# First norm and first modulation group of a hybrid encoder layer: x loaded ahead of the weights, the group summed on TensorE

## The chip, the cores and the metric

One core of a Trainium2 chip runs the kernel; the other seven are idle. The metric is the device time in microseconds, median over runs. Everything is float32 in and out, batch 1, 512 tokens, width 2048.

## The reference, cut to what matters

Only the head of the layer is touched by the change: a modulation vector from c, a normed and modulated copy of x, and the input projection.

```python
mod = silu(c) @ w_ada[l] + b_ada[l]                     # 2048 -> 6 * 2048
sh1, sc1, g1, sh2, sc2, g2 = jnp.split(mod, 6, axis=-1)
h = rms_norm(x, norm_mix_pre[l]) * (1.0 + sc1) + sh1
proj = h @ w_in[l]                                      # then attention heads and HGRN2 heads
...
x = x + g1 * rms_norm(mix, norm_mix_post[l])
h = rms_norm(x, norm_ffn_pre[l]) * (1.0 + sc2) + sh2    # then the convolution FFN
```

For the first norm only sh1 and sc1 are needed: the first 4096 columns of w_ada, 33.5 MB. The gates and the second pair are made later, beside other work.

## The kernel before, in words

All five engines run programs written out by hand; semaphores order them. h is held transposed: 16 row tiles kt of 128 model channels by 512 tokens. A float32 product is made of three passes on TensorE (`three_passes`, L2032 to L2034): each operand is split into a high part (ScalarE copies to a rounded type, lines L742, L776) and a low part (VectorE subtracts, lines L1359, L1355).

**The head of the kernel ("front").** SyncE's queue issues, in order, the rows of w_ada's first 4096 columns (`load_ada`), 16 weight rows w_in of 448 KB (`load_front`), and, between rows 2 to 5 of the first group, the four 1 MB tiles of x. The columns are taken in groups of row tiles, `MOD_GROUPS = ((0, 6), (6, 4), (10, 4), (14, 2))`: group g makes the shift and the scale of its row tiles. A group comes as 16 loads, one for each 128 rows of w_ada. For each, VectorE does ACC = w_ada row * silu(c) + ACC (`add_ada`, L1337 and L1340). After the sixteenth, TensorE sums ACC over its 128 partitions with a matmul against a column of ones for each 128 columns (`sum_ada`, L2027), VectorE adds the bias and forms the scale (`modulate`, L1348, L1350), ScalarE applies both to the transposed x (XN) and makes H_hi (`h_rows`, L772, L776), VectorE makes H_lo (`h_low`, L1355).

**x.** ScalarE squares the four tiles of x (L750), takes the root through Ln and Exp (L752, L753), scales the tiles (L758). TensorE then turns all of x (`turn_x`, L2009, 64 transposes), and ScalarE copies each of the 16 turned row tiles out of PSUM (L763).

**The front rows.** TensorE runs `front_row(kt)` for 16 row tiles, 7 column tiles of three passes each, 21 matmuls of 128x512, with `sum_ada(g)` one row before the first row that needs group g:

```python
sum_ada(0)
for kt in range(KT):
    for g in range(1, len(MOD_GROUPS)):
        if kt == MOD_GROUPS[g][0] - 1:
            sum_ada(g)
    front_row(kt)
```

Five projections of query heads follow at once, then the HGRN2 heads, the output projection and the FFN, all led by TensorE. The raw front weights stand in two slots (W_raw), which come free when VectorE has made the low part. The constants that a reader needs: KT = 16 (row tiles and w_ada rows), TT = 4 (token tiles), RAW = 2 (raw slots), SLOTS = 4 (split weight slots), U_Q = 16 (first unit after the front).

Of the kernel before, what the change touches and what calls it, by code (L numbers as in the profile page):

```python
# [69 lines left out]
MOD_GROUPS = ((0, 6), (6, 4), (10, 4), (14, 2))  # L70
# [80 lines left out]
def hybrid_encoder_layer(nc, x, c, w_ada, b_ada, norm_mix_pre, norm_mix_post, w_in, q_norm, k_norm,  # L151
# [6 lines left out]
    def at(name, shape, dt, offset):  # L158
# [20 lines left out]
    ADA1 = at("ADA1", [P, ADA1_SLOTS, 12 * P], F32, 8 * KB)  # L179
    ADA2 = at("ADA2", [P, ADA2_SLOTS, 8 * P], F32, WK + 32 * KB)  # L180
    ACC = [at("ACC0", [P, 12 * P], F32, WK + 56 * KB), at("ACC1", [P, 8 * P], F32, 56 * KB),
           at("ACC2", [P, 8 * P], F32, WK + 56 * KB), at("ACC3", [P, 4 * P], F32, WK + 62 * KB)]
# [100 lines left out]
    with ExitStack() as ctx:  # L283
# [16 lines left out]
        ada2_landed = [sem(f"ada2_landed{i}") for i in range(ADA2_SLOTS)]  # L300
        ada_added, mod_summed, mod_ready = sem("ada_added"), sem("mod_summed"), sem("mod_ready")
# [78 lines left out]
        OUT_BANKS = [[0, 1, 6, 7], [2, 3, 4, 5]]  # L380

# [68 lines left out]
        def _(sp):  # L450
# [11 lines left out]
            def load_ada(g, r):  # L462

                n = g * KT + r
                row0, rows = MOD_GROUPS[g]
                if g == 0:
                    dst, landed = ADA1[:, r % ADA1_SLOTS, :], ada1_landed[r % ADA1_SLOTS]
                    if r >= ADA1_SLOTS:
                        sp.wait_ge(ada_added, n - ADA1_SLOTS + 1)
                else:  # L470
                    slot = (n - KT) % ADA2_SLOTS
                    dst, landed = ADA2[:, slot, 0:2 * rows * P], ada2_landed[slot]
                    if n - KT >= ADA2_SLOTS:
                        sp.wait_ge(ada_added, n - ADA2_SLOTS + 1)
                sp.dma_start(dst.rearrange("p (s n) -> p s n", s=2),
                             w_ada[0, r * P:(r + 1) * P, 0:2 * D].rearrange("p (s n) -> p s n", s=2)
                             [:, :, row0 * P:(row0 + rows) * P]).then_inc(landed, 16)

            def load_front(u):
                if u >= RAW:  # L480
                    sp.wait_ge(lo_ready, u - RAW + 1)
                sp.dma_start(W_raw[:, u % RAW, 0:FRONT_W], w_in[0, u * P:(u + 1) * P, FRONT_COL:FRONT_COL + FRONT_W])\
                    .then_inc(raw_landed[u % RAW], 16)
# [5 lines left out]
            front = {(0, 0): 0, (0, 1): 1, (0, 9): 2, (0, 10): 3, (1, 0): 4, (1, 1): 5, (1, 13): 6, (1, 15): 7,  # L489
                     (2, 2): 8, (2, 5): 9, (2, 12): 10, (2, 15): 11, (3, 4): 12, (3, 6): 13, (3, 12): 14, (3, 15): 15}  # L490
            for g in range(len(MOD_GROUPS)):
                for r in range(KT):
# [3 lines left out]
                    if g == 0 and 2 <= r < 2 + TT:  # L496
                        sp.dma_start(XT0[:, r - 2, :], x[0, (r - 2) * P:(r - 1) * P, :]).then_inc(x_landed[r - 2], 16)
# [223 lines left out]
        def _(act):  # L721
# [16 lines left out]
            def split_front(u):  # L738
# [3 lines left out]
                act.activation(W_hi[:, u % SLOTS, 0:FRONT_W], W_raw[:, u % RAW, 0:FRONT_W], ACT.Copy).then_inc(hi_ready, 1)  # L742
# [3 lines left out]
            split_front(0)  # L746
            split_front(1)
# [8 lines left out]
            act.wait_ge(x_rstd, 1)  # L756
            for tt in range(TT):
                act.activation(XT0[:, tt, :], XT0[:, tt, :], ACT.Copy, scale=col(SM, RSX + tt)).then_inc(x_scaled, 1)  # L758
                if tt in (1, 3):
                    split_front(2 + tt // 2)  # L760
            for dt in range(KT):
                act.wait_ge(x_turned, dt + 1)
                act.activation(XN[:, dt, :], PB[dt % 4][:, :], ACT.Copy).then_inc(xn_ready, 1)  # L763
# [15 lines left out]
            for u in range(4, 9):  # L779
                split_front(u)  # L780
            h_rows(1)
            for u in range(9, 12):
                split_front(u)
            h_rows(2)
            for u in range(12, 16):
                split_front(u)
            h_rows(3)
            split_hi(0, 2, U_Q)
# [494 lines left out]
        def _(dve):  # L1283
# [14 lines left out]
            dve.memset(col(SM, EPSC), EPS)  # L1298
            dve.memset(CT[:, :], 0.0).then_inc(c_zeroed, 1)
# [24 lines left out]
            def add_ada(g, r):  # L1324

                n = g * KT + r
                if g == 0:
                    src = ADA1[:, r % ADA1_SLOTS, :]
                    dve.wait_ge(ada1_landed[r % ADA1_SLOTS], 16 * (r // ADA1_SLOTS + 1))
                else:  # L1330
                    slot = (n - KT) % ADA2_SLOTS
                    src = ADA2[:, slot, 0:2 * P * MOD_GROUPS[g][1]]
                    dve.wait_ge(ada2_landed[slot], 16 * ((n - KT) // ADA2_SLOTS + 1))
                if r == 0:
                    if g == 2:
                        dve.wait_ge(mod_summed, 1)
# [20 lines left out]
            def front_low(u):  # L1357
                dve.wait_ge(hi_ready, u + 1)
                dve.tensor_tensor(W_lo[:, u % SLOTS, 0:FRONT_W], W_raw[:, u % RAW, 0:FRONT_W],  # L1359
                                  W_hi[:, u % SLOTS, 0:FRONT_W].bitcast(F32), ALU.subtract).then_inc(lo_ready, 1)  # L1360

            for r in range(KT):
                add_ada(0, r)
                if r == 2:
                    vectors()
                if r in (3, 4):
                    front_low(r - 3)
                if r == 10:
                    lower_bounds()
                if r in (12, 14):  # L1370
                    front_low(r // 2 - 4)
            for r in range(KT):
# [3 lines left out]
                if 1 <= r <= 6:  # L1376
                    h_low(r - 1)
                if r in (7, 9, 12, 15):
                    front_low(4 + (7, 9, 12, 15).index(r))
            for r in range(KT):  # L1380
# [614 lines left out]
        def _(pe):  # L1995
# [3 lines left out]
            pe.transpose(PB[2][:, 0:P], CT[:, :], ident[:, :]).then_inc(c_turned, 1)  # L1999
            pe.wait_ge(stage_landed, 17 * 16)  # L2000
# [3 lines left out]

            def turn_x(dt):
                if dt >= 4:
                    pe.wait_ge(xn_ready, dt - 3)
                for tt in range(TT):
                    ins = pe.transpose(PB[dt % 4][:, tt * P:(tt + 1) * P], XT0[:, tt, dt * P:(dt + 1) * P], ident[:, :])  # L2009
                ins.then_inc(x_turned, 1)  # L2010

            pe.wait_ge(c_ready, 1)
            pe.wait_ge(vec_ready, 1)
            pe.wait_ge(x_scaled, TT)
            for dt in range(KT):
# [113 lines left out]
            sum_ada(0)  # L2129
# [400 lines left out]
```

## Time and profile before

| | us |
|---|---|
| median of 3 runs (2381.16 to 2386.85) | 2384.36 |
| the profiled execution | 2380.28 |
| its span, first to last instruction | 2378.5 |
| TensorE busy in the span | 2303.4 (97%) |
| VectorE busy | 1863.6 (78%) |
| ScalarE busy | 1101.8 (46%) |

How to read it: PE is TensorE (PEld its weight loads), DVE VectorE, ACT ScalarE, SP the queue of SyncE. Times within the span are us from its first instruction. "Busy" counts an instruction from start to end, so overlapping ones share time.

### The profile page before, as it was taken

Reading aid. Unit: us, or ns where it says so; the run is one execution under the profiler, and the core shown is the slowest. Engines: PE = TensorE matmul, PEld = TensorE weight load, DVE = VectorE, ACT = ScalarE, POOL = GpSimd, SP = SyncE. Lnnn points to the kernel's source line nnn. Section 1 sums busy time; section 2 is a strip of 40 time slices with the busy share of each in tenths; the row PEclk is TensorE's granted clock in tenths of the full one; section 3 lists DMA queues with packets and bytes.
Section 4 is the critical chain, followed back from the end, with each engine's and each line's share of the span. In section 5 each row is a group of like instructions: output and inputs, shape, how many; then the busy total and the mean of one; then the engine's idle time right before and its main releaser. Section 6 shows DMA issues by size and latency. Waiting matters only on the chain.

```text
span 2378.5 us, 36941 instructions
## 1 busy us (share of the span) xinstructions
PE 2303.4 (97%) x13613; PEld 2026.8 (85%) x13613; DVE 1863.6 (78%) x2393; ACT 1101.8 (46%) x1495; POOL 129.3 (5%) x207
## 2 busy tenths in 40 slices
PE   2899999999999999989999999999999999999998
PEld 2777778888888887878999999999999998888887
DVE  6965667876767872267799999999999999889777
ACT  5356753333333352254444444444444445555554
POOL 1010000000000000000000000000000000001100
PEclk9999999999999999999999999999999999999999
DMA  9952456766666734336555555555555569769966
GB/s 370 335 157 72 145 176 199 226 221 210 207 218 186 238 92 174 98 124 155 143 146 146 144 142 143 143 139 141 144 145 142 142 175 327 254 206 291 273 227 223
DMA packets 374480, 442.46 MB, mean 186 GB/s; under 512 B 14620, under 2 KB 291364, under 8 KB 372096
## 3 DMA queue, kind: packets, MB, share of 16 engines
q1 hardware_dynamic: 354704, 369.74, 48.9%
q0 software_dynamic: 19696, 71.68, 13.1%
q8 instruction: 46, 0.75, 0.1%
q14 instruction: 34, 0.28, 0.0%
HBM read 418.81 MB, written 66.08 MB: 204 GB/s over the span
## 4 chain that ended last, share of the span: by engine, by line
PE 92%; DVE 4%; ACT 2%; DMA 1%; issue 1%; SPq 0%; DVEq 0%; ACTq 0%
PE bank L2032 28%; PE bank L2034 27%; PE bank L2033 27%; PE bank L2189 2%; DMA ADA<-in_w_ada_dram 1%; PE bank L2098 1%; PE bank L2221 1%; DVE ACC L1340 1%; PE bank L2208 1%; PE bank L2089 1%; PE bank L2251 1%; DVE W_lo L1294 0%; PE bank L2027 0%; DVE ZZ L1528 0%; PE bank L2347 0%
## 5 line engine op out<-in xcount | busy, mean ns | idle before, releaser
L2032 PE MATMUL bank<-H_lo,W_hi 128*128 128x256 f32 (+1 forms) x1888 | 659.7, 349 | 3.3 <-DVE H_lo L1355 3.3
L2034 PE MATMUL bank<-H_hi,W_lo 128*128 128x256 f32 (+1 forms) x1888 | 635.0, 336 | 0.0
L2033 PE MATMUL bank<-H_hi,W_hi 128*128 128x256 f32 (+1 forms) x1888 | 634.6, 336 | 0.0
L2032 PEld LDWEIGHTS bank<-H_lo,W_hi 128*128 128x128 f32 x1888 | 359.8, 191 | 42.7 <-issue 7.7
L2033 PEld LDWEIGHTS bank<-H_hi,W_hi 128*128 128x128 f32 x1888 | 359.9, 191 | 39.4 <-issue 7.7
L2034 PEld LDWEIGHTS bank<-H_hi,W_lo 128*128 128x128 f32 x1888 | 359.0, 190 | 37.6
L2032 PE MATMUL bank<-T_lo,W_hi 128*128 128x256 f32 x1280 | 362.3, 283 | 0.0
L2033 PE MATMUL bank<-MGR,W_hi 128*128 128x256 f32 x1280 | 362.2, 283 | 0.0
L2034 PE MATMUL bank<-MGR,W_lo 128*128 128x256 f32 x1280 | 362.2, 283 | 0.0
L1294 DVE TENSOR_TENSOR W_lo<-W_raw,W_hi 128x1024 fp32r<-128x1024 f32 x138 | 168.3, 1221 | 110.4 <-ACT W_hi L735 110.0
L2032 PEld LDWEIGHTS bank<-T_lo,W_hi 128*128 128x128 f32 x1280 | 245.7, 192 | 0.1
L2033 PEld LDWEIGHTS bank<-MGR,W_hi 128*128 128x128 f32 x1280 | 245.7, 192 | 0.0
L2034 PEld LDWEIGHTS bank<-MGR,W_lo 128*128 128x128 f32 x1280 | 245.7, 192 | 0.0
L2032 PE MATMUL bank<-W_lo,GS_hi 128*128 128x512 f32 x616 | 240.0, 390 | 1.6 <-DVE W_lo L1882 1.6
L2033 PE MATMUL bank<-W_hi,GS_hi 128*128 128x512 f32 x616 | 239.7, 389 | 0.0
L2034 PE MATMUL bank<-W_hi,GS_lo 128*128 128x512 f32 x616 | 239.6, 389 | 0.0
L1130 ACT ACTIVATE W_hi<-UB 128x1024 fp32r<-128x1024 f32 x160 | 164.1, 1049 | 148.6 <-DVE UB L1751 95.1
L1739 DVE TENSOR_TENSOR W_lo<-UB,W_hi 128x1024 fp32r<-128x1024 f32 x160 | 195.0, 1220 | 26.9 <-ACT W_hi L1130 26.9
L735 ACT ACTIVATE W_hi<-W_raw 128x1024 fp32r<-128x1024 f32 x138 | 144.8, 1050 | 93.9 <-PE bank L2034 44.3
L1577 DVE SCALAR_TENSOR_TENSOR AB_acc<-AB_raw,SM,AB_acc 128x1024 f32<-128x1024 f32 x120 | 153.7, 1281 | 23.1 <-DMA AB_raw<-in_w_ada_dram 22.1
L1130 ACT ACTIVATE W_hi<-W_raw 128x1024 fp32r<-128x1024 f32 x80 | 84.5, 1056 | 150.6 <-DVE W_raw L1751 98.3
L2032 PEld LDWEIGHTS bank<-W_lo,GS_hi 128*128 128x128 f32 x616 | 115.7, 188 | 26.8 <-DVE W_lo L1882 2.5
(280 smaller groups left out, 3603.4 us busy)
## 6 DMA issues: line engine op xcount, KB each, us to landing
AB_raw<-in_w_ada_dram SPq DMA_DIRECT2D x128, 512.0 KB, 4.5
UB<-in_w_up_dram SPq DMA_DIRECT2D x100, 512.0 KB, 4.1
W_raw<-in_w_in_dram SPq DMA_DIRECT2D x90, 512.0 KB, 4.7
t_dram<-in_w_down_dram POOLq DMA_DIRECT2D x88, 512.0 KB, 7.9
DRAW<-in_w_down_dram SPq DMA_DIRECT2D x66, 512.0 KB, 6.1
W_raw<-in_w_up_dram SPq DMA_DIRECT2D x56, 512.0 KB, 3.9
W_raw<-in_w_down_dram SPq DMA_DIRECT2D x44, 512.0 KB, 6.1
ADA<-in_w_ada_dram SPq DMA_DIRECT2D x32, 512.0 KB, 6.3
```

Of the source, the lines that this page charges most:

```text
L735: act.activation(W_hi[:, k % SLOTS, :], W_raw[:, k % RAW, :], ACT.Copy).then_inc(hi_ready, 1)
L1130: act.activation(units(W_hi[:, (U_ST + PRODUCTS * jj + p) % SLOTS, :]), ST[e][ST_UNIT[p]], ACT.Copy)\
L1294: dve.tensor_tensor(W_lo[:, k % SLOTS, :], W_raw[:, k % RAW, :], W_hi[:, k % SLOTS, :].bitcast(F32), ALU.subtract).then_inc(lo_ready, 1)
L1340: ins = dve.scalar_tensor_tensor(ACC[g][:, :], src, col(SM, CS + r), ACC[g][:, :], ALU.mult, ALU.add)
L1577: ins = dve.scalar_tensor_tensor(AB_acc[:, :], AB_raw[:, kt % 2, :], col(SM, CS + kt), AB_acc[:, :], ALU.mult, ALU.add)
L1739: dve.tensor_tensor(units(W_lo[:, slot, :]), ST[e][ST_UNIT[p]], units(W_hi[:, slot, :].bitcast(F32)), ALU.subtract)\
L2032: pe.matmul(acc, st_hi, mv_lo, start=start, stop=False, skip_group_check=on)
L2033: pe.matmul(acc, st_hi, mv_hi, start=False, stop=False, skip_group_check=on)
L2034: return pe.matmul(acc, st_lo, mv_hi, start=False, stop=stop, skip_group_check=on)
L2089: ins = pe.transpose(PB[6 + qt % 2][:, k * P:(k + 1) * P], PM[qt][:, k * P:(k + 1) * P], ident[:, :])
L2098: ins = pe.matmul(PB[2][:, :], VSA[:, k, :], PT[:, k, :], start=(k == 0), stop=(k == TT - 1))
L2189: ins = pe.matmul(bank[:, a * P:(a + 1) * P], KM[:, a * P:(a + 1) * P], queries, start=True, stop=True)
```

## The change

Five groups in place of four: row tiles (4, 4, 4, 2, 2). The first group is no longer added up by VectorE: for each of its 16 w_ada rows, TensorE multiplies the row's 8 column blocks, as stationary operands, by the matching column of silu(c), and accumulates into 8 columns of PSUM bank 7 (`ada_row`), which a matmul with zeros has opened. The rows 8 to 15 alternate with the transposes of x. VectorE adds only groups 1 to 4. x is loaded ahead of all w_ada rows. VectorE scales x, where ScalarE did. ScalarE's two splits of front units 2 and 3 come behind its copies of the turned x. The raw front weights 2 to 13 have places of their own (FRAW), and their loads wait for the high part of two units before; unit 6 waits for all transposes.

```diff
-MOD_GROUPS = ((0, 6), (6, 4), (10, 4), (14, 2))
+MOD_GROUPS = ((0, 4), (4, 4), (8, 4), (12, 2), (14, 2))
...
     def load_ada(g, r):
-        n = g * KT + r
+        n = (g - 1) * KT + r
         if g == 0:
             if r >= ADA1_SLOTS:
-                sp.wait_ge(ada_added, n - ADA1_SLOTS + 1)
+                sp.wait_ge(ada_used, r - ADA1_SLOTS + 1)
...
     def load_front(u):
         if u >= RAW:
-            sp.wait_ge(lo_ready, u - RAW + 1)
+            sp.wait_ge(hi_ready, u - RAW + 1)
+        if u == RAW + 4:
+            sp.wait_ge(x_turned, KT)
+        if u >= RAW + len(FRAW):
+            sp.wait_ge(lo_ready, u % RAW + 1)
...
+    for tt in range(TT):
+        sp.dma_start(XT0[:, tt, :], x[0, tt * P:(tt + 1) * P, :]).then_inc(x_landed[tt], 16)
+    front = {(0, 0): 0, (0, 1): 1, (0, 10): 2, (0, 12): 3, (1, 4): 4, (1, 5): 5, (1, 9): 6, (1, 13): 7,
+             (2, 0): 8, (2, 8): 9, (2, 11): 10, (2, 14): 11, (3, 2): 12, (3, 8): 13, (3, 14): 14, (4, 5): 15}
...
 ScalarE
-    split_front(0)
-    split_front(1)
+    act.activation(col(SM, RSX), col(SM, EPSC), ACT.Ln)
...
     act.activation(SM[:, RSX:RSX + TT], SM[:, RSX:RSX + TT], ACT.Exp, scale=-0.5).then_inc(x_rstd, 1)
+    split_front(0)
+    split_front(1)
+    for dt in range(KT):
+        act.wait_ge(x_turned, dt + 1)
+        act.activation(XN[:, dt, :], PB[X_BANK + dt % 4][:, :], ACT.Copy).then_inc(xn_ready, 1)
+    split_front(2)
+    split_front(3)
...
-    for tt in range(TT):
-        act.activation(XT0[:, tt, :], XT0[:, tt, :], ACT.Copy, scale=col(SM, RSX + tt)).then_inc(x_scaled, 1)
...
 VectorE
+    dve.wait_ge(x_rstd, 1)
+    for tt in range(TT):
+        dve.tensor_scalar(XT0[:, tt, :], XT0[:, tt, :], col(SM, RSX + tt), None, ALU.mult).then_inc(x_scaled, 1)
+    vectors()
+    for u in range(4):
+        front_low(u)
+    for r in range(KT):
         add_ada(1, r)
         if r == 0:
             modulate(0)
-        if 1 <= r <= 6:
+        if 1 <= r <= 4:
             h_low(r - 1)
+        if r == 5:
+            lower_bounds()
...
+    for r in range(KT):
+        add_ada(4, r)
+        if r == 4:
+            modulate(3)
+        if r == 6:
+            front_low(14)
+        if r in (8, 10):
+            h_low(12 + (r - 8) // 2)
     front_low(15)
+    modulate(4)
...
 TensorE
+    def ada_row(r):
+        row0, rows = MOD_GROUPS[0]
+        pe.wait_ge(ada1_landed[r % ADA1_SLOTS], 16 * (r // ADA1_SLOTS + 1))
+        for sec in range(2):
+            for j in range(rows):
+                o, c = (sec * rows + j) * P, sec * KT + row0 + j
+                ins = pe.matmul(PB[7][:, c:c + 1], ADA1[:, r % ADA1_SLOTS, o:o + P], col(SM, CS + r),
+                                start=False, stop=(r == KT - 1), skip_group_check=True)
+        ins.then_inc(mod_summed if r == KT - 1 else ada_used, 1)
+    pe.wait_ge(c_ready, 1)
+    pe.matmul(PB[7][:, 0:2 * KT], ident[:, :], MOD[:, 0:2 * KT], start=True, stop=True)
+    for r in range(3):
+        ada_row(r)
...
+    for r in range(3, 8):
+        ada_row(r)
     pe.wait_ge(x_scaled, TT)
-    for dt in range(KT):
+    for dt in range(4):
         turn_x(dt)
+    dt = 4
+    for r in range(8, KT):
+        ada_row(r)
+        for n in range(2 - r % 2):
+            turn_x(dt)
+            dt += 1
...
-    sum_ada(0)
```

TensorE's queue before, from the small vectors (STG) to the first front row: all transposes of x in one piece, then the sums of the first group over ACC.

```order
L2002 MATMUL bank<-ident,STG 128x128 x5
L2009 MATMUL bank<-ident,XT_61 128x128 [waits x_scaled,vec_ready,c_ready]
L2009 MATMUL bank<-ident,XT_61 128x128 x15
L2009 MATMUL bank<-ident,XT_61 128x128 [waits xn_ready]
L2009 MATMUL bank<-ident,XT_61 128x128 x3
L2027 MATMUL bank<-ones,ACC_64 128x1 [waits ada_added,xn_ready,consts_landed]
L2027 MATMUL bank<-ones,ACC_64 128x1 x11
L2032 MATMUL bank<-H_lo,W_hi 128x512 [waits lo_ready,h_lo]
```

(The pair of XT rows with the wait for xn_ready comes 12 times there.) TensorE's queue after the change, same place, from row 7 of w_ada to row 9:

```order
L2025 MATMUL bank<-SM,ADA_62 128x1 [waits ada1_landed7]
L2025 MATMUL bank<-SM,ADA_62 128x1 x7
L2015 MATMUL bank<-ident,XT_61 128x128 [waits x_scaled]
L2015 MATMUL bank<-ident,XT_61 128x128 x15
L2025 MATMUL bank<-SM,ADA_62 128x1 [waits ada1_landed0]
L2025 MATMUL bank<-SM,ADA_62 128x1 x7
L2015 MATMUL bank<-ident,XT_61 128x128 [waits xn_ready]
L2015 MATMUL bank<-ident,XT_61 128x128 x3
L2015 MATMUL bank<-ident,XT_61 128x128 [waits xn_ready]
L2015 MATMUL bank<-ident,XT_61 128x128 x3
L2025 MATMUL bank<-SM,ADA_62 128x1 [waits ada1_landed1]
L2025 MATMUL bank<-SM,ADA_62 128x1 x7
```

The 12 sum matmuls behind the transposes have gone, and 16 blocks of 8 matmuls of the same shape (128x128 stationary, one column moving) stand ahead of, between and behind the transposes.

VectorE's queue after the change, from the scaling of x to the second row of group 1 (ACC1); FRAW0 and FRAW1 are raw front weights 2 and 3:

```order
L1372 TENSOR_SCALAR XT0_61<-XT0_61,SM_58 128x2048 [waits x_rstd,c_ready]
L1372 TENSOR_SCALAR XT0_61<-XT0_61,SM_58 128x2048 x3
L1321 COPY VEC_56<-bank0 128x512 [waits vec_turned]
L1367 TENSOR_TENSOR W_lo_52<-W_raw_53,W_hi_51 128x896 [waits hi_ready] x2
L1367 TENSOR_TENSOR W_lo_52<-FRAW0_68,W_hi_51 128x896 [waits hi_ready]
L1367 TENSOR_TENSOR W_lo_52<-FRAW1_69,W_hi_51 128x896 [waits hi_ready]
L1345 TENSOR_SCALAR ACC1_64<-ADA2_63,SM_58 128x1024 [waits ada2_landed0]
L1356 TENSOR_TENSOR MOD_57<-bank7,VEC_56 128x2x4 [waits mod_summed]
L1358 SCALAR_TENSOR_TENSOR SM_58<-MOD_57,VEC_56 128x4 [waits mod_ready]
L1348 SCALAR_TENSOR_TENSOR ACC1_64<-ADA2_63,SM_58,ACC1_64 128x1024 [waits ada_added,ada2_landed1]
```

The 16 adds of the first group are gone from the head of this queue, and the first add of group 1 now stands behind the low parts of units 2 and 3.

## Rows read from the trace of the kernel before

**Rows 1.** The page: busy time of TensorE; the chain's shares by engine.
```profile
PE 2303.4 (97%) x13613; PEld 2026.8 (85%) x13613; DVE 1863.6 (78%) x2393; ACT 1101.8 (46%) x1495; POOL 129.3 (5%) x207
...
PE 92%; DVE 4%; ACT 2%; DMA 1%; issue 1%; SPq 0%; DVEq 0%; ACTq 0%
```

**Rows 2.** Waits of TensorE over the span: total us, times, longest.
```profile
PE bank L2009 <- ACT XT L758: 25.5, 1, 25.5
...
PE bank L2366 <- DVE MG L1665: 7.9, 1, 7.9
PE bank L2027 <- DVE ACC L1340: 7.3, 2, 4.8
...
PE bank L2032 <- DVE Q_lo L1454: 2.0, 1, 2.0
```

**Rows 3.** Chain of waits, 53 to 63 us: start, us, what.
```profile
55.89 3.06 PE bank L2027 x24
...
59.38 1.52 ACT XN L772 x2
60.89 0.53 ACT H_hi L776
...
62.19 0.80 PE bank L2032
```

**Rows 4.** Chain of waits, 0 to 260 us: the sums of the second group.
```profile
87.64 1.69 PE bank L2027 x16
```

**Rows 5.** Timeline of TensorE: start, us, what, count, idle before.
```profile
17.36 1.54 PE L2002 MATMUL bank<-ident,STG 128*128 128x128 f32 x6 [13.24 <-DMA STG<-in_k_norm_dram]
44.41 8.95 PE L2009 MATMUL bank<-ident,XT 128*128 128x128 f32 x64 [25.50 <-ACT XT L758]
...
113.30 3.57 PE L2027 MATMUL bank<-ones,ACC 128*128 128x1 f32 x16 [4.78 <-DVE ACC L1340]
...
137.27 0.95 PE L2027 MATMUL bank<-ones,ACC 128*128 128x1 f32 x8
```

**Rows 6.** Windows: us, PE, PEld, DVE, ACT, POOL busy (count), granted clock, DMA share, GB/s.
```profile
44.00:48.00 4.00, 3.59 (x17) 3.62 (x18) 3.38 (x3) 2.90 (x5) 0.00 (x0) 1.00 1.03 402
48.00:52.00 4.00, 4.00 (x38) 4.00 (x37) 3.90 (x4) 3.90 (x9) 0.00 (x0) 1.00 1.03 398
...
58.40:65.00 6.60, 3.34 (x10) 2.68 (x11) 5.10 (x7) 5.62 (x9) 0.00 (x0) 0.50 1.05 391
113.00:119.60 6.60, 6.30 (x23) 5.73 (x24) 5.09 (x10) 2.30 (x4) 0.00 (x0) 0.50 0.77 243
```

**Rows 7.** Windows over the loading of the first group, same columns.
```profile
5.00:20.00 15.00, 1.54 (x6) 1.14 (x6) 5.68 (x5) 3.90 (x4) 6.35 (x12) 1.00 1.04 388
20.00:44.00 24.00, 0.00 (x0) 0.00 (x0) 17.70 (x19) 17.37 (x16) 0.00 (x0) 1.00 1.02 404
```

**Rows 8.** Windows over groups 1, 2 and 3 on VectorE, same columns.
```profile
55.66:86.80 31.14, 27.66 (x127) 23.28 (x128) 27.12 (x29) 11.29 (x16) 0.00 (x0) 0.89 0.97 342
86.80:115.16 28.36, 23.59 (x113) 19.79 (x111) 26.17 (x27) 8.73 (x12) 0.00 (x0) 0.96 0.95 338
115.16:134.80 19.64, 19.64 (x82) 16.44 (x83) 16.80 (x26) 7.76 (x11) 0.00 (x0) 0.88 0.75 232
```

**Rows 9.** VectorE's groups by shape, 55.6 to 135 us: busy us, mean ns, idle before.
```profile
L1359 DVE TENSOR_TENSOR W_lo<-W_raw,W_hi 128x896 fp32r<-128x896 f32 x11 | 11.8, 1085 | 0.0
L1340 DVE SCALAR_TENSOR_TENSOR ACC<-ADA,SM,ACC 128x512 f32<-128x512 f32 x15 | 11.2, 750 | 1.5 <-DMA ADA<-in_w_ada_dram 0.8
...
L1337 DVE TENSOR_SCALAR ACC<-ADA,SM 128x512 f32<-128x512 f32 x1 | 0.5, 480 | 0.0
```

**Rows 10.** Timeline of ScalarE: a split, and copies of turned row tiles.
```profile
44.17 0.93 ACT L742 ACTIVATE W_hi<-W_raw 128x896 fp32r<-128x896 f32 x1
45.54 0.60 ACT L763 ACTIVATE XN<-bank 128x512 f32<-128x512 f32 x1 [0.43 <-PE bank L2009]
...
48.10 6.49 ACT L763 ACTIVATE XN<-bank 128x512 f32<-128x512 f32 x13 [0.26 <-PE bank L2009]
```

More of the change, by code:

```diff
@@ L178, in hybrid_encoder_layer, with front_raw @@
     XT0 = at("XT0", [P, TT, D], F32, WK)
-    ADA1 = at("ADA1", [P, ADA1_SLOTS, 12 * P], F32, 8 * KB)
+    ADA1 = at("ADA1", [P, ADA1_SLOTS, 8 * P], F32, 8 * KB)
     ADA2 = at("ADA2", [P, ADA2_SLOTS, 8 * P], F32, WK + 32 * KB)
-    ACC = [at("ACC0", [P, 12 * P], F32, WK + 56 * KB), at("ACC1", [P, 8 * P], F32, 56 * KB),
-           at("ACC2", [P, 8 * P], F32, WK + 56 * KB), at("ACC3", [P, 4 * P], F32, WK + 62 * KB)]
+    ACC = [None, at("ACC1", [P, 8 * P], F32, 56 * KB), at("ACC2", [P, 8 * P], F32, WK + 56 * KB),
+           at("ACC3", [P, 4 * P], F32, WK + 62 * KB), at("ACC4", [P, 4 * P], F32, WK)]
+    FRAW = [at(f"FRAW{n}", [P, FRONT_W], F32, 40 * KB + 4 * KB * n if n < 4 else WK + 2 * KB + (n - 4) * 4 * FRONT_W)
+            for n in range(12)]
+    def front_raw(u):
+        return FRAW[u - RAW][:, :] if RAW <= u < RAW + len(FRAW) else W_raw[:, u % RAW, 0:FRONT_W]
     STG = at("STG", [P, 6, P], F32, MXB)
@@ L380, in hybrid_encoder_layer @@
         OUT_BANKS = [[0, 1, 6, 7], [2, 3, 4, 5]]
+        X_BANK = 3
         def g_pair(m):
@@ L778, in _ @@
             h_rows(0)
-            for u in range(4, 9):
+            for u in range(4, 7):
                 split_front(u)
             h_rows(1)
-            for u in range(9, 12):
+            for u in range(7, 11):
                 split_front(u)
             h_rows(2)
-            for u in range(12, 16):
+            for u in range(11, 15):
                 split_front(u)
             h_rows(3)
+            split_front(15)
+            h_rows(4)
             split_hi(0, 2, U_Q)
@@ L1298, in _ @@
             dve.memset(col(SM, EPSC), EPS)
+            dve.memset(MOD[:, 0:2 * KT], 0.0)
             dve.memset(CT[:, :], 0.0).then_inc(c_zeroed, 1)
@@ L1999, in _, with turn_x @@
             pe.transpose(PB[2][:, 0:P], CT[:, :], ident[:, :]).then_inc(c_turned, 1)
+            def turn_x(dt):
+                if dt >= 4:
+                    pe.wait_ge(xn_ready, dt - 3)
+                for tt in range(TT):
+                    ins = pe.transpose(PB[X_BANK + dt % 4][:, tt * P:(tt + 1) * P], XT0[:, tt, dt * P:(dt + 1) * P], ident[:, :])
+                ins.then_inc(x_turned, 1)
+            def ada_row(r):
[11 more added lines that the diff above has]
+                ada_row(r)
             pe.wait_ge(stage_landed, 17 * 16)
```

81 lines of the change are left out of this document (23 added, 58 removed).

## The prediction
> **What bounds the kernel now.** I read the page first, then TensorE's waits, then the chain of waits at the head. TensorE is busy for 97% of the span and makes up 92% of the chain [rows 1]. Its waits are few: 25.5 us for the scaled x and 7.3 us for VectorE's sums lie in the head of the kernel, and behind it 7.9 us at the start of the FFN and 2.0 us are the longest [rows 2]. So whatever the head gains or loses reaches the end whole, and all else can be left out: the change touches nothing behind it.
>
> The head has two parts. Up to 62.19 us TensorE waits for the first modulation group: the sums run from 55.89 us for 3.06 us, ScalarE and VectorE need the rest, and the first front matmul starts at 62.19 [rows 3]. After that TensorE works through the 16 front rows, held up before the third group's sums (4.78 us idle, then 3.57 us of sums), and starts the last group's sums at 137.27 us [rows 5]. Behind these there are 0.95 us of sums and three rows (3 x 21 matmuls at 0.227 us, 14.3 us) before and after the change alike. **The measure of the change is therefore the start of the last sums: 137.27 us now.**
>
> **TensorE's clock at the head.** The 17 transposes between 44 and 48 us took 3.59 us, 0.211 us each; the 38 after 48 us took 4.00, 0.105 each [rows 6]. The clock column reads 1.00 in both, but the spacing says that TensorE is at 1.2 GHz up to 48 us and at 2.4 after; a column that reads 1.00 from 0 us on I take as unrecorded there. It had done next to nothing before 44.41 us. The clock then fell again: 0.50 from 58.40 to 65 us [rows 6], after the transposes had ended at 53.4 us [rows 5] and though the 128x1 sums ran from 55.89 on [rows 3]. It is 0.50 once more from 113.00 to 119.60 [rows 6], and the sums that fill 113.30 to 116.87 do not lift it [rows 5].
>
> **What an ada row costs on TensorE.** One row is 8 matmuls of 128x128 by one column, the shape of the sums. The trace keeps two records for each: the 8 matmuls of the third group are x16. They took 3.57 us at half clock [rows 5], and the second group's 8 took 1.69 us at full clock [rows 4]. A row therefore costs 3.57 or 1.69 us, 16 rows 57.1 or 27.0. The DMA brings a row of 0.524 MB in 1.31 us at 400 GB/s [rows 7]: at either clock TensorE, in order, becomes slower than the loads that it follows.
>
> **Part by part.**
> - Loads. x (4.19 MB) and row 0 (0.52 MB) come first; at 388 GB/s from 5 us [rows 7], with some 0.6 MB moved before, row 0 is there at about 17.5 us (15.8 by bytes, plus landing time). All 16 rows are there at 43 us. Neither x's norm nor its scaling matters then: TensorE asks for the scaled x only behind row 7, at 17.5 + 8 x 3.57 + 1.5 = 47.6 us, 30 us after x has landed, and all that ScalarE did between 20 and 44 us, squares, root and half of the scalings among it, was 17.37 us [rows 7]. VectorE's four scalings, at most 4 x 0.48 = 1.9 us each by a 512-column one [rows 9], the Ln table moved forward and the matmul with zeros lie under the same cover. At full clock it is 14 us wide, and some 2 us might show.
> - TensorE up to the end of row 15 (call it T). 17.5 + 57.1 for rows + 1.5 for the six STG transposes [rows 5] + 15 turned row tiles ahead of it at 0.845 us (4 x 0.211), 12.7. T = 88.8 us at half clock. The sums before ended at 58.95.
> - From T to VectorE's first add of group 1. The last turn (0.85), ScalarE's copy (0.60), the splits of units 2 and 3 (2 x 0.93) [rows 10], and the low part of unit 3 (1.08) [rows 9] stand in a row, because VectorE's queue has those low parts ahead of the adds: 4.4 us, so it starts at 93.2. Before it was 55.66.
> - VectorE from there to the last add. Before: 79.1 us in three windows, 70.1 of them busy [rows 8]. Added: a fourth pass of 16 adds of 512 columns (15 x 0.75 + 0.48) [rows 9], 11.7 us; the lower bounds, moved in here, and one more modulate, about 1.3; low part 14, 1.0. Fewer waits remain to it, since TensorE waits instead: between 84 and 93 us, I take 91. Last add: 184.2 us.
> - TensorE's 16 rows (16 x 21 x 0.227 = 76 us) fit under VectorE's 91 us, so it waits at the sums and starts some of them at half clock, as at 113.30 now; that is 1 to 4 us for the upper end.
> - SyncE. Loading unit 4 waits for ScalarE's split of unit 2, and all of group 1 from row 5 on is queued behind it. It resumes near T + 2.5 with six rows already landed; VectorE needs row 5 nine us later. Nothing.
> - FRAW and the waits on the high part only make loads earlier; VectorE is the later one. Nothing.
>
> **Sum:** 184.2 - 137.27 = 46.9 us later. The profiled execution took 2380.28 us, so 2427; it lies 4 us under the median shown (2384.36), from which it would be 2431. I state 2427. 0.2% (5 us) is about what a measurement of this kernel can tell from no change.
>
> **Rivals.**
> - *The transposes lift the clock for a time.* Before, some 3.6 us of transposes did, and it stayed up about 10 us [rows 6]. After the change the four turns between rows 7 and 8 are 3.4 us in one piece. If the clock then holds for 10 us, what takes 20 at half is done in 10: T = 79, end 37 us later, 2417. Against it: the trace has one such rise only, and here rows of one-column matmuls stand on both sides of the transposes.
> - *TensorE is at full clock throughout.* T = 17.5 + 27.0 + 0.8 + 15 x 0.5 (the 13 copies in 6.49 us set the pace [rows 10]) = 52.8; plus 4.0 and 91 gives 147.8, or 10.6 us later: 2391. For it: TensorE would be without a pause from row 3 on. Against it: the sums at 113.30 ran without a pause at half clock [rows 5]. The Trainium skill, TensorE: Matmul & The Clock Gate, "What's actually happening", says that "the default state is throttled, and activity releases the throttle"; if rows of such matmuls count as activity, this case is what it leads to. By this trace they do not. The same page, "LDWEIGHTS (loading the stationary operand)", prices a load of 128 columns by the columns alone, which gives an estimate of 0.107 us, 1.7 us a row, and so this case's time whatever the clock; the trace agrees at full clock (0.106) and disagrees at half (0.223), and the measurement decides.
> - *Faster.* If an ada row costs TensorE no more than its landing, 1.31 us (0.082 a record; the lowest here is 0.106 [rows 4]), T = 44, and if VectorE also never waits, its 70.1 us busy plus 14 end at 48 + 84 = 132.2: 5 us earlier, 2375. It decides from 1.31 us a row down and needs both.
> - *No change.* The same T with VectorE's waits as now, 48 + 91 = 139: 2 us later, 2382. That is also what is left if moving the first group off VectorE is simply paid back by its fifth pass and its later start.
>
> **Chances.** Half clock all through 0.50 (2427); lifted for a time 0.22 (2417); full clock 0.17 (2391); no change 0.06; faster 0.05. The first three are slower by over 0.2%: 0.89. For the range, 2388 takes in the full-clock case less a few us for shorter waits on VectorE, and 2436 the upper ends: VectorE at 93, sums at half clock, the median 4 us over the profiled execution. Outside are mostly the last two cases.
>
> **What would show it.** In the profile after: blocks of x16 records of 128x1 at about 3.6 us each from 17 us on, with no idle time between them; the last of them ending near 89 us; VectorE idle from about 35 to 85 us; DMA idle in the same stretch, as only eight rows fit; first front matmul near 97 us; TensorE waiting for VectorE's adds ahead of three or four sums; last sums near 184 us. Blocks of 1.7 us mean the full-clock case. The prediction is wrong altogether if the first front matmul starts before 60 us, or if VectorE needs much less than 84 us from its first add of group 1.

## The result, and the profile after

| | before | after |
|---|---|---|
| median of 4 runs, us | 2383.74 (2381.16 to 2386.85) | 2430.97 (2429.11 to 2434.63) |
| the profiled execution | 2380.28 | 2430.45 |
| its span | 2378.5 | 2428.3 |

The changed kernel is slower by 47 us: 1.0202 times the time before, 95% interval 1.0189 to 1.0214. The forecast was 46.9 us (2427 against the profiled execution, 2431 against the median). From one profiled execution to the other it is 50.2 us.

TensorE's timeline up to the first front row (start, us, what, count, idle before). It answers to [rows 5].

```profile
17.59 10.40 PE L2025 MATMUL bank<-SM,ADA 128*128 128x1 f32 x48 [12.22 <-DMA ADA<-in_w_ada_dram]
27.86 1.52 PE L2036 MATMUL bank<-ident,STG 128*128 128x128 f32 x6
29.17 17.07 PE L2025 MATMUL bank<-SM,ADA 128*128 128x1 f32 x80
46.10 3.65 PE L2015 MATMUL bank<-ident,XT 128*128 128x128 f32 x16
49.55 3.41 PE L2025 MATMUL bank<-SM,ADA 128*128 128x1 f32 x16
52.82 1.95 PE L2015 MATMUL bank<-ident,XT 128*128 128x128 f32 x8
...
82.08 3.41 PE L2025 MATMUL bank<-SM,ADA 128*128 128x1 f32 x16
85.35 1.09 PE L2015 MATMUL bank<-ident,XT 128*128 128x128 f32 x4
94.04 0.77 PE L2066 MATMUL bank<-H_lo,W_hi 128*128 128x512 f32 x1 [7.59 <-DVE H_lo L1363]
```

Read it down the left column: from 17.59 us to 86 TensorE does not pause once, and all of it is ada rows and transposes. Rows 3 to 7 are the x80: 17.07 us, 3.41 each. A row and the two turned tiles behind it go from 49.55 to 54.56; the transposes at x8, which take 1.74 us from their start to the next row's and so 0.22 us each, are at 1.2 GHz too ([rows 6] have 0.211 and 0.105 for the two levels). Row 15 ends at 85.35; the first front matmul starts at 94.04, 31.85 us later than before [rows 3].

Three windows (us, PE, PEld, DVE, ACT, POOL busy with counts, granted clock, DMA share, GB/s). The first two are the stretch above; the third is the start of VectorE's first group.

```profile
17.00:47.00 30.00, 29.41 (x139) 29.41 (x140) 8.55 (x13) 4.88 (x7) 0.00 (x0) 1.00 0.85 302
47.00:90.00 43.00, 39.45 (x189) 39.04 (x188) 2.05 (x3) 11.35 (x19) 0.00 (x0) 1.00 0.23 77
89.90:117.30 27.40, 16.74 (x63) 13.38 (x63) 25.70 (x31) 7.87 (x11) 0.00 (x0) 0.97 0.87 314
```

Between 47 and 90 us VectorE has 2.05 us of work and the DMA moves 77 GB/s: both wait for TensorE's rows. Before, VectorE and the DMA were at it nearly without a break here [rows 8]. The clock column reads 1.00 in a stretch whose matmuls are spaced as at half clock, as it did before 48 us in [rows 6]; it cannot be used there.

The chain of waits, from the last row to the last sums:

```profile
87.08 0.85 ACT W_hi L755
87.95 2.09 DVE W_lo L1367 x2
90.04 0.67 DVE ACC L1345
...
117.38 3.57 PE bank L2061 x16
...
187.92 1.05 PE bank L2061 x8
```

The last sums, which the prediction made the measure of the change, start at 187.92 in place of 137.27: 50.65 us later, of a span that is 49.8 us longer. Nothing behind them gained or lost more than 1 us.

Waits of TensorE up to 260 us (total us, times, longest); the first line is the sums that VectorE's adds hold up:

```profile
PE bank L2061 <- DVE ACC L1348: 12.8, 3, 6.6
PE bank L2025 <- DMA ADA<-in_w_ada_dram: 12.2, 1, 12.2
PE bank L2066 <- DVE H_lo L1363: 10.6, 2, 7.6
```

Waits of VectorE from 85 to 190 us:

```profile
DVE W_lo L1367 <- ACT W_hi L755: 54.8, 1, 54.8
DVE ACC L1348 <- DMA ADA<-in_w_ada_dram: 7.9, 7, 2.6
DVE H_lo L1363 <- ACT H_hi L787: 3.2, 3, 1.4
```

Waits of SyncE's queue up to 190 us:

```profile
SPq L494 <- ACT W_hi L755: 69.8, 10, 38.6
SPq L483 <- DVE ACC L1348: 30.7, 33, 2.9
SPq L483 <- PE bank L2025: 24.6, 8, 3.7
```

VectorE stands 54.8 us before the low part of unit 2, at the head of its queue, though the first five rows of its own first group had long been there: SyncE issued them before it stopped for 38.6 us at L494, the load of front unit 4, which waits for ScalarE's split of unit 2. That split stands in ScalarE's queue behind the copies of the turned x, which wait for TensorE.

### The profile page after: what moved, and what is told of

Its sections match the earlier page's. It is cut to its first block, busy times and chain, and to the rows that moved or that the text cites. A ratio compares the mean times of both kernels' runs of the same rounds, so it can differ in the third digit from the quotient of the medians.

```text
span 2428.3 us, 37447 instructions
## 1 busy us (share of the span) xinstructions
PE 2365.6 (97%) x13855; PEld 2086.9 (86%) x13855; DVE 1852.6 (76%) x2400; ACT 1095.2 (45%) x1492; POOL 128.6 (5%) x207
## 3 DMA queue, kind: packets, MB, share of 16 engines
q0 software_dynamic: 19696, 71.68, 12.8%
## 4 chain that ended last, share of the span: by engine, by line
PE 90%; DVE 4%; DMA 2%; ACT 2%; issue 1%; SPq 0%; DVEq 0%; ACTq 0%
PE bank L2066 26%; PE bank L2068 26%; PE bank L2067 26%; PE bank L2025 2%; PE bank L2222 2%; DMA ADA<-in_w_ada_dram 2%; PE bank L2132 1%; PE bank L2254 1%; DVE ACC L1348 1%; DMA AB_raw<-in_w_ada_dram 1%; PE bank L2015 1%; PE bank L2241 1%; PE bank L2123 1%; PE bank L2284 1%; DVE W_lo L1307 0%
## 5 line engine op out<-in xcount | busy, mean ns | idle before, releaser
L2066 PE MATMUL bank<-H_lo,W_hi 128*128 128x256 f32 (+1 forms) x1888 | 661.6, 350 | 10.6 <-DVE H_lo L1363 10.6
```

What stands on the lines that cost most here:

```text
L2066: pe.matmul(acc, st_hi, mv_lo, start=start, stop=False, skip_group_check=on)
```

## The experiments

What was to be settled: that the one-column rows on TensorE cost the time (theory A), and by their clock, and not the fifth group, the new order of loads or VectorE's queue. Each kernel's last sums are the measure; the table sets them beside the time at which VectorE starts its first add of group 1 and the stretch from there to the last sums. "Before" was run again beside each series, and its median differs by up to 3 us between them: the column "before beside it" gives it. How far a kernel lies under the change is therefore worked out from the two distances to "before": 47.2 us for the change, less the kernel's own. Where the plain difference of the medians says something else, it stands behind in brackets.

| kernel | row 15 or last add of group 0 ends | VectorE starts group 1 | from there | last sums | median, us | before beside it | ratio (95%) |
|---|---|---|---|---|---|---|---|
| before | 55.7 | 55.66 | 81.6 | 137.27 | | | 1 |
| after | 85.35 | 89.96 | 98.0 | 187.92 | 2430.97 | 2383.74 | 1.0202 (1.0189 to 1.0214) |
| e1 | 50.4 | 50.31 | 100.4 | 150.70 | 2394.97 | 2381.36 | 1.0056 (1.0039 to 1.0073) |
| e4 | 57.8 | 61.96 | 98.2 | 160.14 | 2402.56 | 2381.36 | 1.0088 (1.0071 to 1.0104) |
| e5 | 82.4 | 52.58 | 114.8 | 167.33 | 2413.28 | 2381.36 | 1.0139 (1.0122 to 1.0156) |
| e6 | 72.8 | 77.40 | 99.8 | 177.24 | 2421.36 | 2384.44 | 1.0156 (1.0133 to 1.0179) |
| e7 | 82.4 | 87.03 | 95.7 | 182.71 | 2426.98 | 2381.36 | 1.0196 (1.0179 to 1.0213) |
| e9 | 53.8 | 57.01 | 94.1 | 151.12 | 2396.05 | 2381.97 | 1.0059 (1.0046 to 1.0073) |

**e1: the first group on VectorE again, all else as in the change.** (x first, five groups, raw weights in own places, VectorE scales x.)

```diff
-    for r in range(3, 8):
-        ada_row(r)
     pe.wait_ge(x_scaled, TT)
-    for dt in range(4):
+    for dt in range(KT):
         turn_x(dt)
...
+    sum_ada(0)
...
+            add_ada(0, 0)
             dve.wait_ge(x_rstd, 1)
...
-            vectors()
-            for u in range(4):
-                front_low(u)
+            for r in range(1, KT):
+                add_ada(0, r)
+                if r == 2:
+                    vectors()
+                if r in (3, 4):
+                    front_low(r - 3)
+                if r in (12, 14):
+                    front_low(r // 2 - 4)
```

> The changed kernel with one part undone: the first group (its four row tiles) is added up by VectorE again and summed against ones, all else as changed (x first, five groups, VectorE scales x, FRAW). Theory A (the 47 us are the 16 blocks of one-column matmuls on TensorE at half clock): VectorE needs some 31 us from 17.5 us on for scaling, vectors, 16 adds of 1024 columns and four low parts, so group 0 is summed near 50 us, group 1 starts near 50 and the last sums come near 140 us: 2385, within 5 us of the kernel before. Theory B (the loss comes from the fifth pass over w_ada and the order of loads): the loss stays, over 2410.

Measured: 2394.97 us, 13.6 over the kernel before, which had 2381.36 there, and so 34 us under the change (36 by the plain medians). That is neither of the two times expected (2385; over 2410). TensorE's timeline, sums and first front matmul:

```profile
50.54 3.54 PE L2047 MATMUL bank<-ones,ACC 128*128 128x1 f32 x16 [16.23 <-DVE ACC L1352]
57.34 0.80 PE L2052 MATMUL bank<-H_lo,W_hi 128*128 128x512 f32 x1 [3.25 <-DVE H_lo L1367]
...
150.70 0.95 PE L2047 MATMUL bank<-ones,ACC 128*128 128x1 f32 x8
```

Most of the loss is the move to TensorE. The first front row even starts 5 us before that of the kernel before, and the end is still 13 us later than before: from its first add of group 1 VectorE takes 100.4 us in place of 81.6. Of these 18.8 us, 11.7 are the fourth pass behind the first; most of the rest is VectorE waiting for w_ada rows, 6.6 us where it was 0.8. In e9, where those waits come to 0.7 us, the stretch is 94.1, 12.5 over that of the kernel before: the pass alone. Theory A had given the stretch 90 us (from 50 to 140), 8 more than before; that half of it was wrong.

**e2: 100 idle transposes ahead of row 0**, so that the clock is up when the rows begin. **e3: e2, and 8 more behind every row.**

```diff
     pe.wait_ge(c_ready, 1)
+    for n in range(100):
+        pe.transpose(PB[2][:, 0:P], ident[:, :], ident[:, :])
```
```diff
     ins.then_inc(mod_summed if r == KT - 1 else ada_used, 1)
+    for n in range(8):
+        pe.transpose(PB[2][:, 0:P], ident[:, :], ident[:, :])
```

> The changed kernel with 100 more transposes of the identity (into a bank that nobody reads then) ahead of the first row, in the stretch in which TensorE waits for its first w_ada row, so that it meets the rows at full clock. Theory A (one-column matmuls do not hold the clock): rows 0 to 2 take 1.7 to 2.2 us each while the clock lasts, then the clock falls and the others take 3.3 us again; row 15 ends 3 to 8 us earlier, 2423 to 2428. Theory C (rows are slow for another reason than the clock): rows 0 to 2 at 3.3 us. Theory E (a clock once lifted stays as long as TensorE has work): all rows at 1.7 us, 30 us earlier, near 2400.

> As the run before it, and eight more transposes of the identity behind every row of the first group: 0.85 us at full clock, 1.7 at half, a row. Theory A: what matters is how much of TensorE's time is wide work. With a third of it transposes the clock may hold or not: if it holds, a row with its transposes takes 2.6 us and row 15 ends near 68 us, 2414; if not, 5.0 us, row 15 near 112 us, 2457. Either shows whether added work that computes nothing can pay here.

Measured: e2 2435.05 and e3 2428.94 us, one run each. TensorE's timeline in e2:

```profile
17.88 1.93 PE L2025 MATMUL bank<-SM,ADA 128*128 128x1 f32 x16
21.18 1.95 PE L2025 MATMUL bank<-SM,ADA 128*128 128x1 f32 x16 [1.38 <-DMA ADA<-in_w_ada_dram]
23.68 3.58 PE L2025 MATMUL bank<-SM,ADA 128*128 128x1 f32 x16 [0.55 <-DMA ADA<-in_w_ada_dram]
...
28.43 17.07 PE L2025 MATMUL bank<-SM,ADA 128*128 128x1 f32 x80
```

and in e3, from the four turns on:

```profile
53.72 3.13 PE L2015 MATMUL bank<-ident,XT 128*128 128x128 f32 x16
56.68 1.84 PE L2025 MATMUL bank<-SM,ADA 128*128 128x1 f32 x16
58.39 1.07 PE L2029 MATMUL bank<-ident 128*128 128x128 f32 x8
...
79.78 1.84 PE L2025 MATMUL bank<-SM,ADA 128*128 128x1 f32 x16
```

In e2 two rows run at 2.4 GHz, at 1.9 us; the third already takes 3.58, and every row behind it 3.4. TensorE also stood still for 1.38 and 0.55 us there, so e2 by itself does not say whether the rows or the pauses let the clock fall; e6, below, has the fall without a pause. What was gained at rows 0 and 1 went into waiting for the next row's landing, so the end of row 15 moved by under 1 us, where 3 to 8 were expected, and the time shows no gain. In e3 the last eight rows all run at 1.84 us. Before 53 us the same eight idle transposes behind each row did not do that: rows 2 and 5 to 7 took 3.41 us, and rows 0, 1, 3 and 4 took 1.95 to 2.75. What differs behind 53 us is the turned tiles, which stand there beside the idle transposes; whether they are the reason was not tested. Row 15 ends at 82.4 us, at neither of the two times expected (68 and 112), and the last sums come at 182.48, 5.4 us earlier than in the change; 228 matmuls that compute nothing did not make the kernel slower.

**e4: the same products with the operands exchanged.** The column of silu(c) is stationary and the row of w_ada moves, 512 wide; the sums come out in one partition, which two copies put in ACC, and the sum over partitions follows.

```diff
-        for j in range(rows):
-            o, c = (sec * rows + j) * P, sec * KT + row0 + j
-            ins = pe.matmul(PB[7][:, c:c + 1], ADA1[:, r % ADA1_SLOTS, o:o + P], col(SM, CS + r),
-                            start=False, stop=(r == KT - 1), skip_group_check=True)
+        ins = pe.matmul(PB[(2, 7)[sec]][0:1, :], col(SM, CS + r), ADA1[:, r % ADA1_SLOTS, sec * S:(sec + 1) * S],
+                        start=(r == 0), stop=(r == KT - 1))
...
+            dve.wait_ge(ada_used, KT)
+            dve.tensor_copy(ACC[0][0:1, 0:S], PB[2][0:1, :])
+            dve.tensor_copy(ACC[0][0:1, S:2 * S], PB[7][0:1, :]).then_inc(row_kept, 1)
...
+    sum_ada(0)
```

> The changed kernel with the operands of the first group's matmuls swapped: the column of silu(c) is stationary, the w_ada row moves, two matmuls of 512 columns per row into one partition of two banks; VectorE copies the 1024 sums into a zeroed tile, which is summed against ones. By the float32 matmul of 512 columns (2 records of 0.43 us at full clock) a row costs 1.74 us at full and 3.5 us at half clock, the same as now at either clock. Theory A (one-column matmuls do not lift the clock, wide ones do): rows at 1.74 us, last row done near 54 us instead of 85, end some 28 us earlier than the changed kernel, near 2402. Theory C (the clock stays low at the head whatever TensorE does, or the cost is the row's weights and not the clock): no gain, 2428 to 2433.

Measured: 2402.56 us, 26 under the change (28 by the plain medians). TensorE's timeline:

```profile
17.89 8.27 PE L2030 MATMUL bank<-ADA,SM 128*1 128x512 f32 x12 [14.42 <-DMA ADA<-in_w_ada_dram]
26.08 0.88 PE L2039 MATMUL bank<-ident,STG 128*128 128x128 f32 x6
26.89 8.74 PE L2030 MATMUL bank<-ADA,SM 128*1 128x512 f32 x20
...
55.98 1.88 PE L2030 MATMUL bank<-ADA,SM 128*1 128x512 f32 x4
```

Three rows take 8.27 us from a standing start; the six small transposes behind them take 0.88 us where they took 1.52, and a row takes 1.75 from then on. Same data, same arithmetic, same engine: only which operand moves, and the clock is up within the first three rows. This is the full-clock case of the rivals, brought about by the form of the instruction.

**e5: all adds of group 1 ahead of the low parts of units 2 and 3** (and the loads of front units 4 to 7 among those of group 2), so that VectorE works while TensorE has the rows.

```diff
-            for u in range(4):
-                front_low(u)
+            front_low(0)
+            front_low(1)
             for r in range(KT):
                 add_ada(1, r)
-                if r == 0:
-                    modulate(0)
...
+            front_low(2)
+            front_low(3)
+            modulate(0)
```

> The changed kernel with VectorE's order and the places of the front loads moved: all 16 adds of group 1 come ahead of the low parts of units 2 and 3, in the stretch of 54.8 us in which VectorE is idle, and units 4 to 7 are loaded in group 2. TensorE's rows are untouched. Theory A (behind the first group VectorE's adds set the pace): 20 us of adds leave the path, TensorE becomes the bound behind its first front row, last sums near 165 us instead of 187.9, 2408. Theory B (behind the first group the DMA or TensorE set the pace): under 5 us gained.

Measured: 2413.28 us, 15 under the change (18 by the plain medians); the last sums come 20.6 us earlier. The sums of the second group run at 106.94 us and no longer wait for adds (1.84 us, at full clock). Row 15 ends at 82.4 in this run, 2.9 us earlier than in the change. So 12 to 18 us of the loss is VectorE standing still behind an instruction that it need not have waited for.

**e6: the loads of x between rows 2 to 5 of group 0 again.**

```diff
-    for tt in range(TT):
-        sp.dma_start(XT0[:, tt, :], x[0, tt * P:(tt + 1) * P, :]).then_inc(x_landed[tt], 16)
...
+        if g == 0 and 2 <= r < 2 + TT:
+            sp.dma_start(XT0[:, r - 2, :], x[0, (r - 2) * P:(r - 1) * P, :]).then_inc(x_landed[r - 2], 16)
```

> The changed kernel with x loaded where it was before, between rows 2 to 5 of the first group. Theory A (TensorE's rows set the pace from the first landing on): row 0 lands near 7 us instead of 17.6, and TensorE's chain of rows starts 10 us earlier; the scaled x is there by 36 us, before the rows 0 to 7 are done (7 + 28.6 + 1.5). Row 15 ends 10 us earlier and so does the kernel: 2421. Rival (x first shortens the head): slower than the changed kernel, 2433 or more.

Measured: 2421.36 us, 10 under the change. TensorE's timeline:

```profile
5.69 10.40 PE L2024 MATMUL bank<-SM,ADA 128*128 128x1 f32 x48 [1.08 <-DMA ADA<-in_w_ada_dram]
...
36.66 3.40 PE L2014 MATMUL bank<-ident,XT 128*128 128x128 f32 x16 [0.53 <-DVE XT L1371]
39.89 1.84 PE L2024 MATMUL bank<-SM,ADA 128*128 128x1 f32 x16
41.60 1.07 PE L2014 MATMUL bank<-ident,XT 128*128 128x128 f32 x8
42.51 2.91 PE L2024 MATMUL bank<-SM,ADA 128*128 128x1 f32 x16
...
46.16 3.41 PE L2024 MATMUL bank<-SM,ADA 128*128 128x1 f32 x16
```

Row 0 starts 11.9 us earlier, and the scaled x is asked for at 36.66 with 0.53 us of waiting. Loading x first bought nothing and kept the engine that sets the pace idle for as long as 4.19 MB take. Rows 8 and 9 also show the rival "lifted for a time": after the four turns one row ran at full clock and one partly, worth some 3 us with the transposes between them. The clock then fell, though TensorE did not pause between 36.66 us and the end of row 15: rows of one column, with turns between them, did not hold it. Of the 10.7 us by which the last sums came earlier, some 8 are thus x. The same rise is seen in e5 and e7, and not in the changed kernel's own trace, where row 8 took 3.41.

**e7: the queue of loads freed.** Front loads wait for the split four units before, not two, on semaphores of their own for each place.

```diff
         if u >= RAW:
-            sp.wait_ge(hi_ready, u - RAW + 1)
+            sp.wait_ge(hi_ready, max(u - 3, 1))
```

> The changed kernel with four semaphores of their own for the loads of front units 2 to 13, so that a load waits for the high part of four units before and not of two. VectorE waited 7.9 us for w_ada rows between its first add of group 1 and the last sums, and SyncE's queue 70 us for ScalarE's splits. Theory D (the front loads at the head of SyncE's queue hold the w_ada rows back): these waits go to 2 us or less and the last sums come 5 to 8 us earlier, 2424. Rival (the DMA itself is behind, 0.87 to 0.94 of its share is used): no change, within 2 us of 2431.

Measured: 2426.98 us, 2 under the change (4 by the plain medians). The intervals of the two ratios overlap, so the time alone does not show a gain; what follows is read from the traces. VectorE's waits from 80 to 190 us:

```profile
DVE H_lo L1366 <- ACT H_hi L790: 5.3, 4, 2.1
DVE MOD L1359 <- PE bank L2064: 3.0, 2, 1.6
DVE ACC L1351 <- DMA ADA<-in_w_ada_dram: 1.4, 2, 1.2
```

VectorE's wait for landings fell from 7.9 us to 1.4, so the front loads in SyncE's queue were what held the rows back. But its stretch fell only from 98.0 to 95.7, since it waits for the other two engines in its place; and the other 2.9 us by which the last sums came earlier are the clock again (row 15 ends at 82.4). What the full queue costs here is some 2 us, not the 5 to 8 expected.

**e8: the kernel before, with the low parts of units 4 to 15 on GpSimd.** If VectorE's work behind the first group sets the end, taking 12 x 1.085 us off it should make the kernel before faster.

```diff
+            for u in range(4, KT):
+                pool.wait_ge(hi_ready, u + 1)
+                pool.wait_ge(lo_ready, u)
+                pool.tensor_tensor(W_lo[:, u % SLOTS, 0:FRONT_W], W_raw[:, u % RAW, 0:FRONT_W],
+                                   W_hi[:, u % SLOTS, 0:FRONT_W].bitcast(F32), ALU.subtract).then_inc(lo_ready, 1)
...
-                if r in (7, 9, 12, 15):
-                    front_low(4 + (7, 9, 12, 15).index(r))
...
```

> The kernel before the change with one thing moved: the low parts of front weights 4 to 15 are made by GpSimd, which is idle there, and not by VectorE. Theory A (VectorE's adds and low parts set the pace behind the first group in the kernel before too): VectorE has 12 us less to do, TensorE's 4.8 us wait before the third group's sums goes, last sums near 130 us instead of 137.3, 2375. Rival (GpSimd is slow at it, or the two engines hinder each other in SBUF): a low part takes over 4.8 us, TensorE's time for a row, and the head gets longer, 2390 or more.

Measured: 2392.11 us against 2381.97, ratio 1.0036 (1.0023 to 1.005). VectorE's adds by shape, up to 150 us (busy us, mean ns, idle before):

```profile
L1346 DVE SCALAR_TENSOR_TENSOR ACC<-ADA,SM,ACC 128x1024 f32<-128x1024 f32 x30 | 50.6, 1688 | 1.9
...
L1346 DVE SCALAR_TENSOR_TENSOR ACC<-ADA,SM,ACC 128x512 f32<-128x512 f32 x15 | 14.8, 985 | 1.0
```

Three of the twelve low parts in GpSimd's timeline, the slowest and the fastest among them:

```profile
71.97 3.32 POOL L666 TENSOR_TENSOR W_lo<-W_raw,W_hi 128x896 fp32r<-128x896 f32 x1 [60.74 <-ACT W_hi L748]
...
102.50 2.40 POOL L666 TENSOR_TENSOR W_lo<-W_raw,W_hi 128x896 fp32r<-128x896 f32 x1 [5.99 <-ACT W_hi L748]
114.79 2.08 POOL L666 TENSOR_TENSOR W_lo<-W_raw,W_hi 128x896 fp32r<-128x896 f32 x1 [9.89 <-ACT W_hi L748]
```

and two adds in VectorE's, one while GpSimd is idle and one beside the low part at 102.50:

```profile
67.85 1.28 DVE L1346 SCALAR_TENSOR_TENSOR ACC<-ADA,SM,ACC 128x1024 f32<-128x1024 f32 x1
...
102.84 3.14 DVE L1346 SCALAR_TENSOR_TENSOR ACC<-ADA,SM,ACC 128x1024 f32<-128x1024 f32 x1
```

The 512-column add went from 0.750 us [rows 9] to 0.985, and the 1024-column one takes 1.688 on average, where the kernel before has 1.282 for its 30. GpSimd is two to three times as slow at the low part (2.08 to 3.32 us), but below the 4.8 us that the rival had named. What came true of the rival is its other half: VectorE's adds are longer while GpSimd works, by 15.7 us in all (12.1 and 3.6), more than the 13 us (12 x 1.085) of which VectorE was relieved. The last sums start at 148.77 us, 11.5 later than in the kernel before. Whether the kernel before would gain from less work on VectorE is therefore left open by e8.

**e9: e4, e6 and e7 together**, with rows 0 to 11 ahead of all transposes and four turned tiles before each of rows 12 to 15.

```diff
-    for r in range(3, 8):
+    for r in range(3, 12):
         ada_row(r)
     pe.wait_ge(x_scaled, TT)
-    for dt in range(4):
-        turn_x(dt)
-    dt = 4
-    for r in range(8, KT):
+    for r in range(12, KT):
+        for dt in range(4 * r - 48, 4 * r - 44):
+            turn_x(dt)
         ada_row(r)
-        for n in range(2 - r % 2):
-            turn_x(dt)
-            dt += 1
```

> The changed kernel with three of the changes tried together: the w_ada row as moving operand, x loaded between rows 2 to 5, semaphores of their own for front loads; rows 0 to 11 of the first group now stand ahead of all transposes, four row tiles of which stand ahead of each of rows 12 to 15. Theory A: row 15 ends near 52 us, 6 us earlier than with the moving row alone (2402.6), because TensorE starts at 6 us and not at 18, and the freed queue gives 4 more: 2392. It stays behind the kernel before by the fifth pass of adds (11.7 us of VectorE). Rival (the gains overlap, as VectorE and the DMA are then the bound): 2398 to 2402.

Measured: 2396.05 us, between the two expectations, 33 under the change (35 by the plain medians) and still 14 over the kernel before. TensorE's timeline at the end of the rows and at the last sums:

```profile
6.80 7.61 PE L2032 MATMUL bank<-ADA,SM 128*1 128x512 f32 x12 [3.45 <-DMA ADA<-in_w_ada_dram]
...
51.89 1.88 PE L2032 MATMUL bank<-ADA,SM 128*1 128x512 f32 x4
...
151.12 1.05 PE L2061 MATMUL bank<-ones,ACC 128*128 128x1 f32 x8 [1.13 <-DVE ACC L1350]
```

The last sums come where e1 has them, 151.12 and 150.70, though one sums the first group on TensorE and the other on VectorE. With the rows no longer in the way VectorE's passes over groups 1 to 4 set the end, 94.1 us from a start that cannot come before the group 0 rows are done. No version run here is faster than the kernel before. Undoing the fifth group alone was not tried: with four groups and a small first one, the accumulators need other places in memory than either kernel has.

## Why the prediction was right

The forecast case came, with its mechanism, and its errors were of opposite sign: T came 3.4 us earlier than the sum had it and VectorE's stretch was 6.9 us longer, which with 0.2 between them leaves the last sums 3.7 us later than forecast. That the forecast of 46.9 us and the 47.2 between the medians agree to 0.3 is luck; between the two profiled executions, on which the sum was worked out, it is 50.2.

- **The measure.** "The start of the last sums": 50.65 us later, span 49.8 longer. That nothing behind them matters held in the experiments: the median's distance from the kernel before was that of the last sums to within 0.3 us in e1, e7 and e9, and to within 3.1 in e4, e5 and e6 (3.4 in the change itself). A median of several executions is set against the trace of one there.
- **The first row** at 17.5: 17.59.
- **A row at half clock** at 3.57: from its start to the start of what follows it took 3.27 to 3.42, since 3.57 had been read off a block that counts its last matmul's tail. The 16 rows took 53.4 us and not 57.1, and the turns 0.4 more than their 12.7; that is most of the 3.4 us by which T was set too late (88.8 for 85.35). That rows leave the clock down was right: all 16 blocks ran at half clock, and in e6 and e7 it fell again within two rows of its rise. The Trainium skill, TensorE: Matmul & The Clock Gate, "What's actually happening", says that activity releases the throttle. The trace of e4 agrees, at 1.75 us a row with 512 columns moving; that of the change does not, at 3.41 with one column and no pause from 17.59 us to 86.
- **T to VectorE's first add** 4.4: 4.6 (85.35 to 89.96).
- **VectorE from there to the last add** at 91: 97.9. Its work was well estimated (82.5 us busy in the four windows of the groups; 70.1 and 14 had been forecast), its waits were not. The term that was mis-sized is "FRAW and the waits on the high part only make loads earlier; VectorE is the later one. Nothing": SyncE issues in order, each front load waits for a split of ScalarE's, and the w_ada rows behind it wait with it. Beside the stop of 38.6 us there are nine such stops, 31.2 us together, and seven adds waited 7.9 us for landings, the first of them at 119.99 us, in group 2. The term "SyncE ... Nothing", on the long stop before unit 4, held: no add of group 1 waited for a landing, though five of its rows were there and not six. By e7 only some 2 us of the 7 come from the queue alone; the rest would have been waits for TensorE and ScalarE anyway, which the sum had put at 7 and which are more.
- **First front matmul** near 97: 94.04. "Three or four" sums held up: three, 12.8 us.
- **The rivals.** "Full clock throughout" was off in the change and true of e4, where T came to 57.8 against 52.8 worked out: its price was 21 us over the kernel before, not 10.6, because the clock needed three rows to rise and VectorE took 98 us again. "Lifted for a time" did not come in the change's trace; in e5, e6 and e7 it did, for one to two rows and some 3 us where the rival had 10. "Faster" asked for 1.31 us a row and no waits on VectorE; the best row here is about 1.7 (e3, e4, from start to start), and VectorE took 94 us or more in every kernel with five groups. "No change" did not come; e1 shows that even with the first group where it was, the rest of the change costs 13 us.

Where the 47 us lie by undoing one thing at a time: 34 to 36 the rows on TensorE (e1), of which 26 to 28 go with the form of the matmul (e4); 12 to 18 by letting VectorE's adds go ahead (e5); 8 to 10 x first (e6); some 2 the queue, by the traces (e7). They overlap and do not add up: each cuts the same path at another place. The 13 us left in e1 are a stretch of VectorE's that is 18.8 us longer, 11.7 of them the added pass, less a start 5.4 us earlier. The part of the added pass is worked out from the traces; no run takes it away alone.

## What to carry to other kernels

Before putting a product with one column on TensorE, see whether its operands can be exchanged so that the long side moves: the same 16 rows took 53 us of TensorE one way and 31 the other (8.27 + 8.74 + 8 x 1.8), because the clock rose in the one and not in the other. Before moving work off an engine, ask what stands at the head of that engine's queue afterwards: here VectorE was freed of the first group's adds, 20 us as e1 has them (15 x 1.28 + 0.75), and then stood still for 54.8 us behind a low part. And a smaller first group that starts sooner pays for itself only if the extra pass over the others has a place to hide.

## What was unexpected of the hardware

- Rows of one-column matmuls let a raised clock fall: in e6 a row took 1.84 us, the next 2.91 and the one after 3.41, with turns between them and no pause of TensorE.
- Idle transposes, 8 behind each row, together with the turned tiles held the clock up for eight rows at 1.84 us each (e3, one run), at no cost to the end; behind rows 0 to 7, where no turned tiles stand, they did not.
- GpSimd beside VectorE lengthened VectorE's 512-column add by 31% and its 1024-column one by 32% on average, one of them from 1.28 to 3.14 us, and took 2.1 to 3.3 us for what VectorE does in 1.085 (e8).
